# Other steps for the scores, turns and values of the first eight heads, and another order inside a step

## What is computed

```
h = rms_norm(x); q, k, v, z = split(h @ w_in1)
q = rms_norm(q per head) * 64**-0.5;  k = rms_norm(k per head)
s = q @ k.T - slope[h] * (t - u)        # -inf where u > t
o = softmax(s) @ v
x = x + (o * silu(z)) @ w_out1
```

## Time and profile before

| | |
|---|---|
| median of 3 runs | 326.87 us (326.83 to 327.97) |
| the profiled execution, its own time | 326.89 us |
| its span, first to last instruction | 325.1 us |
| PE busy | 320.1 us, 98% of the span |
| DVE busy | 261.4 us, 80% |
| ACT busy | 236.7 us, 73% |
| share of PE in the chain that ended last | 97% |
| granted TensorE clock, mean | 1.000 |

### The profile page before, as it was taken

The page is one execution under the profiler, slowest core; times in us unless marked ns, Lnnn a source line. Parts: engine busy times, 40 slices in busy tenths (PEclk is TensorE's granted clock), DMA queues, the critical chain, the costliest instruction groups (busy, mean ns, idle before and its releaser), DMA issues.

```text
span 325.1 us, 5845 instructions
## 1 busy us (share of the span) xinstructions
PE 320.1 (98%) x2238; PEld 294.0 (90%) x2238; DVE 261.4 (80%) x484; ACT 236.7 (73%) x439; POOL 51.3 (16%) x58
## 2 busy tenths in 40 slices
PE   8999999999999999999999999999999999999995
PEld 7899999999999999998999999988877777778885
DVE  2799989999999999998895899746555877758533
ACT  4787999997999998997766588434666767566630
POOL 0050024422324112211000000004500231400000
PEclk9999999999999999999999999999999999999999
DMA  7988478989999499987549244971545323200003
GB/s 270 421 315 339 142 252 228 203 152 339 342 335 227 86 375 347 212 260 146 251 137 400 113 132 144 354 277 35 223 138 191 125 95 119 113 2 0 2 1 131
DMA packets 12844, 64.80 MB, mean 199 GB/s; under 512 B 1424, under 2 KB 1552, under 8 KB 6544
## 3 DMA queue, kind: packets, MB, share of 16 engines
q1 hardware_dynamic: 8064, 53.78, 44.5%
q0 software_dynamic: 4608, 10.49, 17.4%
q10 hardware_dynamic: 144, 0.15, 0.2%
HBM read 52.88 MB, written 1.05 MB: 166 GB/s over the span
## 4 chain that ended last, share of the span: by engine, by line
PE 97%; DMA 1%; DVE 0%; ACT 0%; issue 0%
PE bank L1083 27%; PE bank L1084 26%; PE bank L1085 26%; PE bank L1143 4%; PE bank L1117 4%; PE bank L1191 2%; PE bank L1295 2%; PE bank L1322 2%; PE bank L1308 2%; PE bank L1160 1%; DMA X<-xT 1%; PE bank L1274 1%; DVE X L965 0%; ACT scratch L474 0%; PE bank L1206 0%
## 5 line engine op out<-in xcount | busy, mean ns | idle before, releaser
L746 DVE TENSOR_TENSOR w_lo<-raw,w_hi 128x1024 fp32r<-128x1024 f32 x80 | 95.0, 1219 | 15.1 <-ACT w_hi L466 14.8
L466 ACT CAST w_hi<-raw 128x1024 fp32r<-128x1024 f32 x88 | 88.5, 1048 | 5.3 <-PE bank L1085 4.1
L1083 PE MATMUL bank<-h_hi,w_hi 128*128 128x256 f32 x304 | 86.6, 285 | 0.0
L1085 PE MATMUL bank<-h_hi,w_lo 128*128 128x256 f32 x304 | 86.0, 283 | 0.0
L1084 PE MATMUL bank<-h_lo,w_hi 128*128 128x256 f32 x304 | 86.0, 283 | 0.0
L1084 PEld LDWEIGHTS bank<-h_lo,w_hi 128*128 128x128 f32 x304 | 58.3, 192 | 0.1
L1083 PEld LDWEIGHTS bank<-h_hi,w_hi 128*128 128x128 f32 x304 | 58.3, 192 | 0.1
L1085 PEld LDWEIGHTS bank<-h_hi,w_lo 128*128 128x128 f32 x304 | 58.3, 192 | 0.0
L1083 PE MATMUL bank<-ya_hi,w_hi 128*128 128x256 f32 x160 | 46.9, 293 | 0.0
L1084 PE MATMUL bank<-ya_lo,w_hi 128*128 128x256 f32 x160 | 45.2, 282 | 0.0
L1085 PE MATMUL bank<-ya_hi,w_lo 128*128 128x256 f32 x160 | 45.2, 282 | 0.0
(11 more groups left out here) (105 smaller groups left out, 507.2 us busy)
## 6 DMA issues: line engine op xcount, KB each, us to landing
raw<-w SPq DMA_DIRECT2D x49, 1024.0 KB, 6.1
side_v<-side_ring POOLq DMA_DIRECT2D x24, 256.0 KB, 6.9
w_lo<-raw POOLq DMA_DIRECT2D x8, 512.0 KB, 7.4
X<-xT SPq DMA_DIRECT2D x2, 512.0 KB, 5.1
out<-X SPq DMA_DIRECT2D x4, 256.0 KB, 2.6
consts<-const SPq DMA_DIRECT2D x1, 290.0 KB, 13.4
params<-vec ACTq DMA_DIRECT2D x1, 149.0 KB, 4.9
```

The source lines that it names most:

```text
L466: nc.scalar.copy(halves(w_hi, cut_slot(n), half), halves(raw, n % RAW, half)).then_inc(hi_cut, 1)
L746: nc.vector.tensor_tensor(halves(w_lo, cut_slot(n), half), halves(raw, n % RAW, half), halves(w_hi, cut_slot(n), half).bitcast(F32), ALU.s ...
L1083: nc.tensor.matmul(dst, wh, ah, start=start, stop=False, skip_group_check=True)
L1085: return nc.tensor.matmul(dst, wl, ah, start=False, stop=stop, skip_group_check=True)
```

## The change

For the first octet the pairs now follow at ten steps instead of eight. The turn stands seven steps behind the scores on PE instead of eight, and the values ten steps behind instead of eleven. So scores stand at steps 3, 13, 23, 33 (before 3, 11, 19, 27), turns on PE at 10, 20, 30, 40 (before 11, 19, 27, 35) and values at 13, 23, 33, 43 (before 14, 22, 30, 38). Before, a pair's turn fell into the step of the next pair's scores; now its values do. The second octet's steps are as they were. On PE alone, scores are now issued ahead of turns and values of the same step. DVE and ACT follow the new steps by the same table.

```diff
-PAIR_TIMES = (8, 7, 11, 3), (6, 6, 10, 13)
+PAIR_TIMES = (10, 6, 10, 3), (6, 6, 10, 13)
...
             def attention_step(s):
 
+                times = [pair_steps(octet) for octet in range(2)]
                 for octet in range(2):
-                    scores, turns, values = pair_steps(octet)
+                    scores, turns, values = times[octet]
                     for i in range(4):
                         if s == scores[i]:
                             pair_scores(4 * octet + i)
+                for octet in range(2):
+                    scores, turns, values = times[octet]
+                    for i in range(4):
                         if s == turns[i] + 1:
                             pair_turn(4 * octet + i)
                         if s == values[i]:
```

## The result

The changed kernel takes 327.99 us, the median of 16 runs (327.74 to 328.79), against 327.03 us for the kernel before in runs beside it (326.81 to 327.97). The ratio is 1.0031, with a 95% interval of 1.0023 to 1.0038: 1.0 us slower. The forecast was 327.7 us, 0.8 us slower. Both lie inside the half per cent under which the prediction expected a measurement to tell little from no change; with sixteen runs on each side the interval is clear of 1. The span of the profiled execution grew from 325.1 to 326.0 us.

A forecast was written before the change was run, and what follows sets the result against it. PE was taken as the bound: in the changed stretch no matmul waits, so only its own issue or a new wait counts. 326.89 - 0.57 (saving) + 1.40 (wait) = 327.7 us; 8-in-10 range 326.1 to 328.7.

The forecast's parts named there:

- PE itself saves 0.57: First octet on PE: extra cost of blocks falls from 10.89 to 10.32 us, one form change saved in each of three.
- Rival 3: Scores to values on PE: the two split forms follow without a drain, saving 1.3, wait as forecast, 327.0 us; chance 0.05.
- The wait at the second turn, 1.40: Second pair's turn: PE arrives 6.57 us after the scores, its data from DVE at about 8.0, a new 1.40 us wait.
- The sum: Whole kernel: 326.89 - 0.57 saved + 1.40 waited = 327.7 us; chance 0.70.
- The cause within the wait: Second pair on DVE: the cut, now ahead of the scales, idles from 2.70 to 4.50 us for ACT's cast.
- The other pairs pass: Turns of first, third and fourth pairs: data come in time, no wait; the fourth has 0.4 us in hand.
- Rival 2: Fourth turn or PSUM bank handovers (steps 28, 30, 32): PE waits 0.6 us more, 1.2 at two places; 328.9 us; chance 0.12.
- The last values beside the transpose of Q cost nothing: Step 43 on PE: the last values stand next to a transpose of Q, counted as no extra cost.
- heads low of the fourth pair is covered: Second octet: this 0.34 us of DVE costs nothing because an exp on ACT runs beside it; 0.34 if cover fails.

The follow-up runs named there:

- the table alone: The kernel before with only the new table of steps, old order inside a step (values ahead of next pair's scores): 329.97 us, ratio 1.0087; second time 330.29 us, 1.0098.

## Why the prediction was right

By its own steps:

- *PE itself saves 0.57.* Right in cause, and short in size: it saves 0.75. The blocks were priced well: three joint ones save 0.6. Scores to values was taken as 0.86 and is 0.85. What the Trainium skill says (TensorEngine Tiling (Array Packing), Key Properties), that a change of tiling mode drains the engine, agrees with that 0.85. Rival 3 (no drain between the split forms) asked for a step of about 0.6 and is out. What the sum lacked is the 0.12 outside the blocks. With the wait taken away in two different ways the kernel is 0.8 and 0.6 us faster than before; with the joint blocks taken away as well it is level with it.
- *The wait at the second turn, 1.40.* Right in place, cause and nearly in size: 1.50. From the start of the scores, worked out and then measured: gate 1.81 and 1.80, heads high 2.25 and 2.26, exp 2.55 and 2.57, cast 3.45 and 3.46, cut 4.50 and 4.52, end of the second scale 7.97 and 7.99. What was missing is small: 0.06 from the end of the scale to the turn's start, which no row of before showed because no turn waited there, and 0.02 each at the two ends. A turn that had to wait also takes 0.63 to the next matmul instead of 0.57. With these the wait costs 1.50 + 0.06 = 1.56, and 1.56 - 0.75 = 0.81 us, against 0.84 in the trace and 1.0 (0.8 to 1.2) by the ratio.
- *The sum.* 1.40 - 0.57 = 0.83 is almost exactly the 0.84 of the trace. That closeness is in part luck: saving and cost were each too small by some 0.17, and the two errors cancel.
- *The cause within the wait.* The sum put the cut's wait for the cast at 1.80; it is 1.76, and moving that one cast removes the whole loss.
- *The other pairs pass.* Right; the nearest was the fourth, with 0.4 in hand by my sum and 0.23 in the trace (the scale ends at 279.21 + 0.56 = 279.77, the turn starts at 280.00). Rival 2 was that close. DVE, then PE:

```profile
279.21 0.56 DVE L1002 TENSOR_SCALAR scratch<-scratch 128x128 f32<-128x128 f32 x2
```
```profile
280.00 0.81 PE L1308 MATMUL bank<-consts,scratch 128*128 128x128 f32 x6
```

- *The last values beside the transpose of Q cost nothing, heads low of the fourth pair is covered.* Right: no wait appears there, and PE's time behind the stretch is that of before.

Not foreseen, though nothing in this change depended on it: that a longer wait at this place may cost more than itself, as the table alone showed.

## What to carry to other kernels

Where one engine is busy to the end, price a reordering twice: what it saves on that engine, from the distances between starts, and what reserve it takes from the chain that feeds it, by walking that chain through every engine in program order. Look for the instruction that is not part of the chain but stands in its queue (here a weight cut on DVE that waits for a cast on ACT): the repair is to move the cast ahead, or the chain ahead of the cut. Either turned 1.0 us of loss into 0.6 to 0.8 us of gain.

## What the runs showed of the hardware

- One change of the matmul's form fewer saved 0.2 us a block: 1.05 for scores alone and 1.00 for values alone, 1.85 for both together. The block of scores took as long to values (64*128 to 128*64, 0.85 from start to start) as to a projection matmul (64*128 to 128*128, 0.86).
- Behind a gap of 2.44 us between two matmul starts the granted clock fell to 0.50 some 0.6 us after the second start and stood there until about 4 us after it. Matmuls of 512 columns followed each other at 0.43 us instead of 0.23, which cost 1.57 us. Behind gaps of 1.73 and 2.34 us it stayed at 1.00 in the profiles.
